# Moving columns read in short runs from two halves, in one up and one down projection

## The reference

```
u = h @ w_up                          # 1024 -> 2 x 2816
uc = conv_b + sum(conv_w[j] * up[:, j:j + S] for j in range(3))   # causal, depthwise
gate, val = uc[..., :D_FF], uc[..., D_FF:]
return (silu(gate) * val) @ w_down    # 2816 -> 1024
```

## Time and profile before

| | |
|---|---|
| median of 3 runs | 1033.48 us (1033.25 to 1033.53) |
| span of the profiled execution, first to last instruction | 1032.5 us |
| TensorE busy with matmuls | 1027.5 us, 7472 matmuls |
| VectorE, ScalarE, GpSimd busy | 869.8, 687.6, 354.2 us |
| granted TensorE clock | full over the whole span |
| first MLP, TensorE's stretch | about 276 to 456 us |
| second MLP | about 569 to 750 us |
| third MLP | about 848 to 1029 us |

### The profile page before, as it was taken

The page is one execution under the profiler, slowest core; times in us unless marked ns, Lnnn a source line. Parts: engine busy times, 40 slices in busy tenths (PEclk is TensorE's granted clock), DMA queues, the critical chain, the costliest instruction groups (busy, mean ns, idle before and its releaser), DMA issues.

```text
span 1032.5 us, 21155 instructions
## 1 busy us (share of the span) xinstructions
PE 1027.5 (100%) x7472; PEld 959.0 (93%) x7472; DVE 869.8 (84%) x1596; ACT 687.6 (67%) x1263; POOL 354.2 (34%) x370
## 2 busy tenths in 40 slices
PE   9999999999999999999999999999999999999998
PEld 8999999999999999999999899999998998999998
DVE  7877788777799988887776999988897869999886
ACT  7766767666766665676776766665697767566563
POOL 4222221212255633341210555433341014654332
PEclk9999999999999999999999999999999999999999
DMA  8644454446376655526454566655434436665541
GB/s 302 240 161 154 153 185 147 144 162 232 137 234 202 215 193 199 169 94 213 129 190 146 164 218 198 212 186 199 158 117 140 164 123 205 206 217 191 199 163 41
DMA packets 57749, 183.34 MB, mean 178 GB/s; under 512 B 6352, under 2 KB 9680, under 8 KB 57424
## 3 DMA queue, kind: packets, MB, share of 16 engines
q1 hardware_dynamic: 56816, 181.52, 52.9%
q10 hardware_dynamic: 864, 0.92, 0.3%
HBM read 181.36 MB, written 1.05 MB: 177 GB/s over the span
## 4 chain that ended last, share of the span: by engine, by line
PE 97%; DMA 1%; DVE 1%; ACT 0%; POOL 0%; issue 0%; SPq 0%; DVEq 0%; POOLq 0%
PE ps L434 23%; PE ps L436 12%; PE ps L683 9%; PE ps L685 9%; PE ps L684 9%; PE ps L1778 6%; PE ps L1780 6%; PE ps L1779 6%; PE ps L1250 2%; PE ps L1252 2%; PE ps L1251 2%; DMA w_raw<-w_stream 1%; PE ps L868 1%; PE ps L913 1%; PE ps L842 1%; PE ps L880 1%
## 5 line engine op out<-in xcount | busy, mean ns | idle before, releaser
L402 DVE TENSOR_TENSOR w_lo<-w_raw,w_hi 128x1024 fp32r<-128x1024 f32 (+2 forms) x369 | 439.8, 1208 | 30.0 <-ACT w_hi L394 29.4
L394 ACT ACTIVATE w_hi<-w_raw 128x1024 fp32r<-128x1024 f32 (+2 forms) x369 | 353.4, 972 | 117.2 <-PE ps L436 99.8
L434 PE MATMUL ps<-xg,w_hi 128*128 128x512 f32 x1056 | 363.6, 390 | 0.0
L436 PE MATMUL ps<-xg,w_lo 128*128 128x256 f32 x1056 | 291.8, 276 | 0.0
L434 PEld LDWEIGHTS ps<-xg,w_hi 128*128 128x128 f32 x1056 | 198.2, 188 | 40.4 <-DVE w_lo L402 0.8
L436 PEld LDWEIGHTS ps<-xg,w_lo 128*128 128x128 f32 x1056 | 198.2, 188 | 0.0
L1901 POOL TENSOR_TENSOR prob_t<-prob_t,qkT 128x256 f32<-128x256 f32 x63 | 108.1, 1716 | 259.1 <-ACT prob_t L1824 259.1
L683 PE MATMUL ps<-w_hi,xg 128*128 128x384 f32 (+1 forms) x556 | 192.3, 346 | 0.0
L685 PE MATMUL ps<-w_hi,xg 128*128 128x384 f32 (+1 forms) x556 | 187.4, 337 | 0.0
L684 PE MATMUL ps<-w_lo,xg 128*128 128x384 f32 (+1 forms) x556 | 185.6, 334 | 0.0
L1778 PE MATMUL ps<-g_hi,w_hi 128*128 128x256 f32 x528 | 146.0, 276 | 0.0
(11 more groups left out here) (189 smaller groups left out, 1383.0 us busy)
## 6 DMA issues: line engine op xcount, KB each, us to landing
w_raw<-w_stream SPq DMA_DIRECT2D x228, 512.0 KB, 4.1
w_raw<-w_stream SPq DMA_DIRECT2D x137, 384.0 KB, 3.3
w_raw<-w_stream SPq DMA_DIRECT2D x4, 392.0 KB, 3.0
con<-consts SPq DMA_DIRECT2D x1, 1024.0 KB, 7.3
x_all<-x_t SPq DMA_DIRECT2D x4, 256.0 KB, 4.9
conv_taps<-taps SPq DMA_DIRECT2D x1, 1024.0 KB, 7.8
w_raw<-w_stream SPq DMA_DIRECT2D x4, 192.0 KB, 5.7
x_all<-x_a SPq DMA_DIRECT2D x3, 256.0 KB, 6.7
```

Source lines behind the costliest of these rows:

```text
L394: nc.scalar.activation(w_hi[s][:, 0:w], w_raw[s][:, 0:w], ACT.Copy).then_inc(w_hi_done, 1)
L402: nc.vector.tensor_tensor(w_lo(c)[:, 0:w], w_raw[s][:, 0:w], w_hi[s][:, 0:w].bitcast(F32), ALU.subtract).then_inc(w_lo_done, 1)
L434: nc.tensor.matmul(bank(b, 0, 2 * TOK), w_hi[s][:, k * P:(k + 1) * P], xg[:, k, :, :].rearrange("p h t -> p (h t)"), start=(k == 0), stop= ...
L436: last = nc.tensor.matmul(bank(b), w_lo(c)[:, k * P:(k + 1) * P], xg_hi[:, k, :], start=False, stop=(k == KT - 1), skip_group_check=True)
```

## The change

A table gives every tile index a run length: none for 0 and 7, then 4, 8, 16, 32, 64 and 2 for 1 to 6. For a tile with a run length, `in_runs` rewrites an operand of 2H columns so that it is taken as: the first run of the first half, the first run of the second half, the second run of the first half, and so on. The moving operand and the output are rewritten alike, so that every column lands where it did. It is applied to the wide up matmul (L434) in the second MLP (index k), and to the three down matmuls (L1778 to L1780) in the first MLP (index m). The two halves of an up operand are x_hi and x_lo (256 columns each), those of a down operand are tokens 0 to 127 and 128 to 255. Stationary operands, waits, increments and their order are as before.

```
+    RUNS = (None, 4, 8, 16, 32, 64, 2, None)
+
+    def in_runs(x, run):
+
+        return x if run is None else x.rearrange("p (a t c) -> p t a c", a=2, c=run)
+
     def project2_k(eng, c, b, k):
         s = c % RING
-        nc.tensor.matmul(bank(b, 0, 2 * TOK), w_hi[s][:, k * P:(k + 1) * P], xg[:, k, :, :].rearrange("p h t -> p (h t)"),
+        run = RUNS[k] if FFN_C0[1] <= c < FFN_C0[1] + 3 * FT else None
+        nc.tensor.matmul(in_runs(bank(b, 0, 2 * TOK), run), w_hi[s][:, k * P:(k + 1) * P],
+                         in_runs(xg[:, k, :, :].rearrange("p h t -> p (h t)"), run),
                          start=(k == 0), stop=False, skip_group_check=True)
...
                     first = i is None and j == 2 and m % 2 == 0
-                    nc.tensor.matmul(acc(m), wh, g_hi[b][:], start=first, stop=False, skip_group_check=True)
-                    nc.tensor.matmul(acc(m), wh, g_lo[b][:], start=False, stop=False, skip_group_check=True)
-                    last = nc.tensor.matmul(acc(m), wl, g_hi[b][:], start=False, stop=True, skip_group_check=True)
+                    run = RUNS[m] if f == 0 else None
+                    out, hi, lo = in_runs(acc(m), run), in_runs(g_hi[b][:], run), in_runs(g_lo[b][:], run)
+                    nc.tensor.matmul(out, wh, hi, start=first, stop=False, skip_group_check=True)
+                    nc.tensor.matmul(out, wh, lo, start=False, stop=False, skip_group_check=True)
+                    last = nc.tensor.matmul(out, wl, hi, start=False, stop=True, skip_group_check=True)
```

## The result

The changed kernel takes 1050.16 us (median of 4 runs, 1049.85 to 1051.59) against 1033.51 us of the kernel before in the same series: 16.65 us more, a ratio of 1.0165 with a 95% interval of 1.0153 to 1.0177. The execution that was profiled is the longest of the four, 1051.59 us; the other three took 1049.85 to 1050.16. The forecast of no change, 1033.5, was wrong; the stated range, 1029 to 1053, holds the time.

What follows compares the result with a forecast made beforehand. TensorE was taken as the bound, busy 1027.5 of 1032.5 us. The terms summed to 0 on that span; with the median of the runs 1.0 above it, the forecast was 1033.5 us, range 1029 to 1053.

Steps and rivals of the forecast that it cites:

- What bounds the kernel: Whole kernel: TensorE, busy 1027.5 us of 1032.5, with three waits of 1.8 us; what one column costs is the whole question.
- The gain: Touched matmuls in both MLPs become quicker than before; chance 0.09, and the range from 1029 leaves out its fuller half.
- I take nothing: Middle estimate for the broken column order in the touched matmuls of both MLPs: 0 us; no price had chance 0.47.
- Theory F: From the experiments: moving reads pay four cycles per opened four-column group; its other pair is free next, later two or four.
- The rival of the short runs: Touched tiles: short runs starve the column stream; run 2 alone at half pace costs 15.8 us; chance 0.22, with runs of 4 0.03.
- The rival of the slower cadence: Touched matmuls fall to 350 ns an up pair and 120 ns a down matmul, 5.3 us in all; chance 0.13.
- The rival of the output side: Broken PSUM writes put all six touched tiles at half pace, 94.8 us, giving 1128.3; chance 0.06.
- the starved run of 2: Tile 6 in both MLPs, run 2 alone at half pace: 15.8 us, giving 1049.3; chance 0.22 for 1049 to 1051.

## Why the prediction was right and wrong

*What bounds the kernel* was right: it is TensorE, with three waits of 1.8 us in all before and two of 1.6 after. The 18.1 us by which the two stages grew came through in full.

*The gain* did not come: no kernel here was faster than the one before, and the lowest ratio was 0.9998 (0.9989 to 1.0008), with broken writes. The chance of 0.09 and the end of the range at 1029 count on matmuls quicker than before. No run shows such a term: the middle values of the contiguous tiles are 226 to 227 ns for 512 columns and 113 to 114 for 256, 0.44 ns a column, or more.

*"I take nothing"* is the step that failed, and it carried the forecast: the price of the broken order was put at 0 and measured 16.65 us. The 0 was the author's estimate, and no row showed it. In its place the runs showed that a tile in runs of 2 from two streams takes 320 ns for 512 columns, 1.25 ns for two columns where contiguous ones take 0.89, some 7.5 us in both stages. Theory F would put this down to groups of four that are each opened once and visited twice. For longer runs the 0 was nearer: 64 is free (ratio 1.0004), but 4 and 8 cost 11 to 24 ns of 227 in tiles behind a contiguous one.

*The rival of the short runs* had the right side and the wrong size: half pace for the tile of 2, 15.8 us, against 7.5 measured, since some 70% of the pace is left (227 of 321 ns) and not a half. Its total, 1049.3, lies near the result by luck: it has one cost at twice its size and not the other. Its signature, pairs of tile 6 at 545 ns and triples at 650, came as 444 and 497.

*The rival of the slower cadence* was taken as an alternative; it came in addition. Sized at 5.3 us, it came to 9 or 10, since it also took hold of matmuls that weren't touched: the L444 of every tile, tiles 0 and 7, and the down projection of the second MLP, in whole or in part. The prediction had charged only the 660 touched ones. Its mark, the same cadence whatever the run length, is about what tiles 3 to 5 and 7 show. That it lies in how the streams of columns and weights stand to each other was the author's estimate; the runs show only that it moves with the place of the low weights (113 to 118 ns).

*The rival of the output side* is excluded by the kernel that only writes in runs. Its 94.8 us were half pace, the prediction's own size for it; measured was a ratio of 0.9998.

That the range held is luck too: it was drawn up to the starved run of 2, at a pace that did not come, and the slower cadence filled the rest.

What stays open: whether runs of 16 and 32 cost anything of their own (they were only run beside shorter ones); why eight streams cost more than four; what price runs of 4 and 8 would have in tiles that are all alike; why the untouched matmuls fell back to 113 ns in some profiles and stayed long in others; by what the address of the low weights acts; and why a contiguous tile takes 227 ns where theory F gives 213.

## What to carry to other kernels

Where TensorE is the bound, break the moving operand into runs of 64 columns, which were free here (ratio 1.0004). If it must be shorter, take whole aligned groups of four f32r columns (241 to 255 ns for 512 columns against 227 in runs of 4, 238 to 242 in runs of 8), and not pairs from several places (317 to 509 ns). An output in PSUM in runs of 2 to 64 from two halves cost nothing (ratio 0.9998), so a reordering that is needed belongs there. And compare matmuls by the distance of their starts, tile by tile, the untouched ones too: the duration of a contiguous matmul stayed at 0.28 to 0.29 us while its cadence went from 113 to 124 ns.

## What the runs showed of the hardware that I had not expected

The place of the low weights in SBUF changes the pace of contiguous matmuls: moved by 64 to 128 bytes they made the kernel 1.7 to 2.1% slower (1051.69 and 1054.96 us), with the same instructions and no new wait. The pace of a matmul also depends on the ones before it: behind a tile in runs of 2, contiguous matmuls of 256 columns took up to 128 ns instead of 113, and behind runs of 2 from eight places 159. And a moving stream with two columns in each group of four runs at half pace though it goes steadily upwards (437 to 442 ns for 512 columns).
